# Gated recurrence in the scan stage: its input product and its output sum on GpSimd, the running sum left on VectorE

## What the reference computes

```
rg = sigmoid(block_diag_linear(xc, wa, ba))
ig = sigmoid(block_diag_linear(xc, wx, bx))
log_a = -8 * rg * softplus(-lam)
a  = exp(log_a)
bt = sqrt(-expm1(2 * log_a)) * (ig * xc)
h[t] = a[t] * h[t-1] + bt[t]          # in each direction; latents start from the context's last h
out  = (h_forward + h_backward) * gelu(gb) @ w_proj_lru
```

## Time and profile before

| what | value |
|---|---|
| median of 3 runs | 4300.68 us (4300.09 to 4311.89) |
| the profiled execution: time, span | 4309.31 us, 4307.5 us |
| granted TensorE clock, mean share of full speed | 0.93 |
| busy over the span: PE, DVE, ACT, POOL | 83%, 56%, 44%, 29% |
| scan stage | 1142 to 2402 us, a body every 66 to 73 us |

### The profile page before, as it was taken

One profiled execution on the slowest core, in us unless ns is written; L12 is line 12 of the kernel. 1 busy time (PEld: TensorE's weight loads), 2 busy tenths in 40 slices (PEclk: granted clock), 3 DMA queues, 4 the chain that ended last, 5 costly groups with the idle time before them and its releaser, 6 DMA issues. The chain is left out here.

```text
span 4307.5 us, 117683 instructions
## 1 busy us (share of the span) xinstructions
PE 3596.5 (83%) x50061; PEld 3199.9 (74%) x50061; DVE 2432.9 (56%) x4389; ACT 1889.2 (44%) x3285; POOL 1258.8 (29%) x1250
## 2 busy tenths in 40 slices
PE   5799999999677777877777588894599999999992
PEld 2678888888577676777667488672499999999992
DVE  3237676510156666677767654435666666666664
ACT  3246665521154555555555443331244444444444
POOL 2223333311254655555553254000001010101110
PEclk8899999999898999999999799996699999999996
DMA  5235555532433333332331574431367676767675
GB/s 173 69 127 180 170 185 168 171 111 71 117 72 83 93 82 83 83 92 79 87 96 35 175 229 142 147 127 40 115 196 221 195 219 198 214 203 209 208 207 196
DMA packets 566343, 610.18 MB, mean 142 GB/s; under 512 B 65938, under 2 KB 471252, under 8 KB 564820
## 3 DMA queue, kind: packets, MB, share of 16 engines
q1 hardware_dynamic: 515540, 487.01, 36.9%
q0 software_dynamic: 21536, 76.56, 6.2%
q10 hardware_dynamic: 28768, 39.16, 2.8%
HBM read 443.09 MB, written 159.40 MB: 140 GB/s over the span
## 5 line engine op out<-in xcount | busy, mean ns | idle before, releaser
L339 DVE TENSOR_TENSOR moe_w_lo<-moe_w_lo_whole,moe_w_hi 128x2048 fp32r<-128x2048 f32 (+1 forms) x258 | 453.6, 1758 | 263.5 <-ACT moe_w_hi L517 188.0
L460 PE MATMUL moe_h<-moe_xt_hi,moe_w_hi 128*128 128x256 f32 x2048 | 582.0, 284 | 15.9 <-DVE moe_xt_lo L339 14.8
L460 PE MATMUL moe_h<-moe_xt_lo,moe_w_hi 128*128 128x256 f32 x2048 | 580.1, 283 | 0.6 <-issue 0.6
L460 PE MATMUL moe_h<-moe_xt_hi,moe_w_lo 128*128 128x256 f32 x2048 | 580.1, 283 | 0.0
L1792 PE MATMUL inward_pp<-u_u_hi,inward_w_hi 128*128 128x512 f32 (+1 forms) x1360 | 527.4, 388 | 20.8 <-POOL inward_w_lo L1952 20.8
L1792 PE MATMUL inward_pp<-u_u_lo,inward_w_hi 128*128 128x512 f32 (+1 forms) x1360 | 515.7, 379 | 0.0
L1792 PE MATMUL inward_pp<-u_u_hi,inward_w_lo 128*128 128x512 f32 (+1 forms) x1360 | 515.5, 379 | 0.0
L460 PEld LDWEIGHTS moe_h<-moe_xt_hi,moe_w_hi 128*128 128x128 f32 x2048 | 393.2, 192 | 27.9 <-issue 23.7
L460 PEld LDWEIGHTS moe_h<-moe_xt_lo,moe_w_hi 128*128 128x128 f32 x2048 | 393.3, 192 | 3.7
L460 PEld LDWEIGHTS moe_h<-moe_xt_hi,moe_w_lo 128*128 128x128 f32 x2048 | 393.3, 192 | 1.1 <-issue 0.8
L412 POOL DMA_INDIRECT scratch_x<-moe_ys,moe_who x32 | 70.6, 2205 | 912.2 <-DVE moe_ys L568 907.4
(11 more groups left out here) (374 smaller groups left out, 9832.1 us busy)
## 6 DMA issues: line engine op xcount, KB each, us to landing
moe_w_lo_whole<-in_moe_w SPq DMA_DIRECT2D x387, 512.0 KB, 5.0
scratch_ops<-inward_ops SPq DMA_DIRECT2D x72, 514.0 KB, 3.8
scan_over<-scratch_ops SPq DMA_DIRECT2D x72, 512.0 KB, 9.9
inward_w_lo_whole<-in_w_in SPq DMA_DIRECT2D x38, 512.0 KB, 4.6
scan_aq<-scratch_ops SPq DMA_DIRECT2D x36, 516.0 KB, 5.0
scratch_gates<-inward_out SPq DMA_DIRECT2D x64, 256.0 KB, 2.2
all_late<-in_w_mod POOLq DMA_DIRECT2D x32, 512.0 KB, 4.5
rest_modsum<-scratch_gates SPq DMA_DIRECT2D x64, 256.0 KB, 4.4
```

What stands on the lines that cost most here:

```text
L339: return nc.vector.tensor_tensor(x_lo, x, x_hi.bitcast(F32), ALU.subtract)
L460: mm = nc.tensor.matmul(hb[ft % 2][m][:, 0:CAP], w_, x, start=(k == 0 and part == 0), stop=(k == KD - 1 and part == 2))
```

## The change

ScalarE's square root gets a scale of 0.25, so that the factor 0.5 of the "in" product is inside the root. The "in" product moves to GpSimd (`inputs`), as a plain product; the copy or addition into `z` moves to GpSimd (`summed`); VectorE's `recur` keeps the scan. New waits: the scan for the product, the output sum for the scan, ScalarE's `gates`, `squares` and `store_z` for the output sum. GpSimd's loop is written in another order. The diff, cut to its core:

```
-        DVs, POl = lru("scanned", ["in", "scan", "add"]), lru("pool", ["large", "one"])
+        DVs, POl, POi, POz = lru("scanned", ["scan"]), lru("pool", ["large", "one"]), lru("inputs", ["in"]), lru("summed", ["add"])
...  (gates, squares and store_z on ScalarE)
-                    DVs.wait(act, "scan", k - RING)
+                    POz.wait(act, "add", k - RING)
...
-                    act.activation(root[:, a:e, :], root[:, a:e, :], ACT.Sqrt).then_inc(s_root, 1)
+                    act.activation(root[:, a:e, :], root[:, a:e, :], ACT.Sqrt, scale=0.25).then_inc(s_root, 1)
...
             def store_z(j):
-                DVs.wait(act, "add", 2 * NG * (j + 1) - 1)
+                POz.wait(act, "add", 2 * NG * (j + 1) - 1)
...  (recur on VectorE)
-                dve.wait_ge(s_root, sum(1 + (4 * it % RING > 2) for it in range(k // 4 + 1)))
-                DVs.did("in", dve.scalar_tensor_tensor(out=x, in0=gated[:, k % RING, :], scalar=0.5, in1=x, op0=ALU.mult, op1=ALU.mult))
-                DVs.wait(dve, "in", k)
+                POi.wait(dve, "in", k)
+                if m:
+                    DVs.wait(dve, "scan", k - 1)
...
                 DVs.did("scan", dve.tensor_tensor_scan(x[:, way], decay[:, k % RING, way], x[:, way], start, ALU.mult, ALU.add))
...
-                    DVs.did("add", dve.tensor_copy(piece, h))
-                else:
-                    DVs.did("add", dve.tensor_tensor(piece, piece, h, ALU.add))
...  (new on GpSimd)
+            def inputs(k):
+                x = root[:, k % RING, :]
+                pool.wait_ge(s_root, sum(1 + (4 * it % RING > 2) for it in range(k // 4 + 1)))
+                POi.did("in", pool.tensor_tensor(x, x, gated[:, k % RING, :], ALU.mult))
+            def summed(k):
+                DVs.wait(pool, "scan", k)
+                if d == 0:
+                    POz.did("add", pool.tensor_copy(piece, h))
+                else:
+                    POz.did("add", pool.tensor_tensor(piece, piece, h, ALU.add))
...
+                more, first, past = it <= LAST, 4 * (it - 1), 4 * (it - 2)
+                squares(first)
+                inputs(past)
+                inputs(past + 1 if past >= 0 else -1)
                 if more:
                     start_solve(it)
-                squares(first)
+                    level(1, it)
+                summed(past)
+                summed(past + 1 if past >= 0 else -1)
                 if more:
                     level(2, it)
                 squares(first + 1 if it else -1)
+                inputs(past + 2 if past >= 0 else -1)
+                inputs(past + 3 if past >= 0 else -1)
                 if more:
                     level(3, it)
+                summed(past + 2 if past >= 0 else -1)
+                if more:
                     level(4, it)
                 squares(first + 2 if it else -1)
                 if more:
                     level(5, it)
+                summed(past + 3 if past >= 0 else -1)
                 squares(first + 3 if it else -1)
```

More of the change, by code:

```diff
@@ L2151, in scan @@
         none = n.sb("none", [P, 4])
+        spare = n.sb("spare", [P, 1])
         level_pe = [x for m in LEVELS for x in (f"F{m}", f"W{m}", f"T{m}")][:-1]
@@ L2784, in level @@
                     PO[u].did(f"H{m}", pool.tensor_tensor(four(H[u][(m - 1) % 3][:, :, :]), four(L[u][:, :, :]), masked(f"lev{m}t"), ALU.mult))
+            def inputs(k):
+                if k < 0:
+                    return
+                x = root[:, k % RING, :]
+                pool.wait_ge(s_root, sum(1 + (4 * it % RING > 2) for it in range(k // 4 + 1)))
+                POi.did("in", pool.tensor_tensor(x, x, gated[:, k % RING, :], ALU.mult))
+            def summed(k):
+                if k < 0:
+                    return
+                j, d, m, i = lru_of(k)
+                x = root[:, k % RING, :]
+                DVs.wait(pool, "scan", k)
+                if m == 0:
+                    POz.did("add", pool.memset(spare[:, :], 0.0))
+                    return
+                piece = z.rearrange("p (r w) -> p w r", w=GRID_W)[:, 8 * i:8 * i + 8, :]
+                h = x.rearrange("p (w r) -> p w r", r=GRID_H)
+                if d == 0:
+                    if m == 1 and j:
+                        pool.wait_ge(s_z, 16 * j)
+                    POz.did("add", pool.tensor_copy(piece, h))
+                else:
+                    POz.did("add", pool.tensor_tensor(piece, piece, h, ALU.add))
             def squares(k):
@@ L2796, in _ @@
                 PO[u].start(pool)
-            POl.start(pool)
+            for s in (POl, POi, POz):
+                s.start(pool)
             pool.wait_ge(s_masks, 16)
@@ L2801, in _ @@
             for it in range(LAST + 2):
-                more, first = it <= LAST, 4 * (it - 1)
+                more, first, past = it <= LAST, 4 * (it - 1), 4 * (it - 2)
+                squares(first)
+                inputs(past)
+                inputs(past + 1 if past >= 0 else -1)
                 if more:
                     start_solve(it)
-                squares(first)
+                    level(1, it)
+                summed(past)
+                summed(past + 1 if past >= 0 else -1)
                 if more:
-                    level(1, it)
                     level(2, it)
                 squares(first + 1 if it else -1)
+                inputs(past + 2 if past >= 0 else -1)
+                inputs(past + 3 if past >= 0 else -1)
                 if more:
                     level(3, it)
+                summed(past + 2 if past >= 0 else -1)
+                if more:
                     level(4, it)
@@ L2819, in _ @@
                         count = add(2 * it + half, count)
+            for k in range(4 * LAST, 4 * LAST + 4):
+                inputs(k)
+            for k in range(4 * LAST, 4 * LAST + 4):
+                summed(k)
 def backbone_layer(nc, t, out, scratch):
```

## The result

| | before | after |
|---|---|---|
| median (range), us | 4303.47 (4300.09 to 4311.89), 6 runs | 4332.69 (4321.43 to 4338.76), 6 runs |
| ratio with 95% interval | | 1.0057 [1.0043, 1.0071] |
| span and granted clock of the profiled execution | 4307.5 us, 0.932 | 4327.9 us, 0.923 |

The change costs 0.57%, 25 us of 4305. That is more than the 13 us that the prediction took as "no change". By the ratio it is inside the prediction's range of 4272 to 4330 (4300.7 x 1.0057 = 4325); the bare median, 4332.69, lies 2.7 us above it.

The account below looks back on a forecast made before the run. No engine is full in the scan stage; a body is a chain of waits through several queues. 15 bodies x (-1.0 - 0.2 + 1.2) = 0, and +3 once, on 4300.7: 4304 us, range 4272 to 4330.

Parts of the forecast that it names:

- rival C: GpSimd's queue becomes the bound: output sum takes 1.5 us or more, delaying q3 and T update by 2.0; 4328; chance 0.16.
- The stall absorbs part of the relief: First half of a body: of the 2.0 us wait for Z removed, -1.0 us a body survives TensorE's stall before chunk 2.
- H1 costs at most 0.3 us ... and the wait of unit 1 covers that: First half, GpSimd's H1 behind products and four additions: at most 0.3 us on unit 0, covered; uncovered, 0.5 us a body.
- The second half, +1.2 a body: After VectorE's S update, q3 waits for GpSimd's output sum, H4 and `squares`; W update late: +1.2 us a body, range +0.6 to +2.0.
- The output sum: GpSimd's copy or addition into z, price unknown: 0.9 us taken, 1.5 the upper bound for the addition.
- Taps, -0.2: VectorE's chunk 0 taps run with GpSimd idle, giving back the 3.3 us Lk wait: -0.2 us a body.
- `store_z`, +3 once: `store_z` of k = 35 holds ScalarE until the sum of a body's last piece, behind H5: once some 3 us.
- Its point of decision: The GpSimd-queue rival decides from the point at which q3 starts more than 1.2 us late.
- Rival D: Lock between engines: VectorE's two-input operations stretch while GpSimd works beside taps of chunks 1 and 3; +12 us, 4316; chance 0.10.

Follow-up runs that it names:

- sum_behind: The changed kernel with the third piece's output sum behind H4 and `squares` in GpSimd's queue instead of ahead of them: 4318.89 us, 1.0018 to the kernel before.
- relief_only: The kernel before with input product and output sum left out on every engine, z zeroed once: 4299.6 us, 0.9977 to the kernel before.
- small_load_relief: The kernel before with the operand reload cut to 16 columns per tile, and input product and output sum left out: 4183.5 us, 0.9701 to before.
- dummies: The kernel before, VectorE's work whole, plus GpSimd in the changed order doing products and plain copies on private tiles: 4324.39 us, 1.0025 to before.
- placed: The changed kernel with products 1, 2 back on VectorE, GpSimd's other new work behind H4 and H5, `store_z` two chunks later: 4312.37 us, 0.9997 to before.

## Why the prediction was right or wrong

It said 4304, no change by its bound. By the ratio the kernel came to 4325: inside the range, but 25 us slower than before, beside rival C's 4328. The range held by errors in both directions, and the number of C was met without its reason, so that is in part luck. The ledger in us, predicted and measured; sum_behind and relief_only share a chip:

| term | predicted | measured | from |
|---|---|---|---|
| relief, with the taps | -18 | -10 | relief_only |
| GpSimd's new work apart from q3: H1, contention | 0 | +18 | sum_behind over relief_only |
| q3 and the W update late | +18 | +17 | after over sum_behind |
| `store_z` | +3 | not seen apart | |
| sum | +3 | +25 | |

The measured terms are steps from one kernel to the next, so they add up by construction; each has an interval of 4 to 8 us to each side.

- **The stall absorbs part of the relief: right, undersized.** -1.0 a body was taken, the middle of 0 and -2.0; S2 came 0.7 sooner, and all of the relief is worth 10 / 15 = 0.67. That it absorbs is shown by small_load_relief. The Trainium skill ("Runtime: NRT & Kernel Launch", Instruction fetch mechanics) has block crossings mostly hidden, and by it the term would have been -2.0. The relief was worth 1.5 a body only where the reload was small.
- **"H1 costs at most 0.3 us ... and the wait of unit 1 covers that": this step failed.** The prices of the products were right (742 ns for 0.8), and the additions behind them begin 13.5 us into the body, as worked out. But the four additions were priced at 1.26 each, 5.0 together, and take 5.8 from the first to the last (means 1447 and 1491 ns, 1278 and 1277 before). H1 is done at 20.7 and 22.1 us of the body, not at 1706.0 - 1686.2 = 19.8 and 21.1. So F1 waits 11.8 us in all for H1, starts 0.5 a body later than before, and S1 is reached 1.0 later than in relief_only. That the relief took the cover away is not the reason: in dummies, without relief, F1 waits 12.6. The prediction named 0.5 a body for a missing cover and gave it no chance. Whether the delay costs time is another matter: in dummies the stall takes it back before S2.
- **The second half, +1.2 a body: the wait was foreseen, its size about right.** The order of GpSimd's queue, q3's start (5.91 us after the S update for 5.7 to 6.0) and F4's wait are as described. The W update is 9.71 - 8.07 = 1.64 later, where 8.9 - 7.5 = 1.4 was worked out for one body and 1.2 taken. Two errors in that partly cancel: the mark of before was one body with 7.5 (the mean is 8.07), and q3 was priced at 0.45 where it takes 1.43 beside an H product. S2 to S3 got 1.83 longer, 1.40 of it F4's wait. The low clock in 8 of 15 bodies, which the prediction never considered, is a small part of the rest. Over the whole kernel sum_behind shows 17 us for the term of 18: close, with part of what S2 to S3 lose not arriving at the end.
- **The output sum: sized right.** 0.9 was taken, 733 and 999 ns were measured.
- **Taps, -0.2:** the group fell from 135.9 to 131.2 us and TensorE's wait for Lk is not in the list, but the last part of the body (S3 to the end) got 0.25 longer, within its scatter, so no gain is seen to arrive.
- **`store_z`, +3 once:** ScalarE stands for it in three bodies, not one, 4.0 to 5.2 us each and 9.3 us more in all than before. What of that reaches the time, no run shows: placed issues it later and changes more besides.
- **Rival C** had the number and not its reason: the output sum is not 1.5 us or more. Its point of decision, q3 over 1.2 us late, was passed: 5.91 - 4.53 = 1.4.
- **Rival D** is in the result as a part. The Trainium skill ("SBUF — State Buffer", two separate sides) has an exclusive lock held for a whole instruction. The rows agree that operations stretch on both sides (q3 515 to 925 ns, T0 and W0 from 1278 to 1447 and 1491), and VectorE got back all the busy time that it gave. Its price on the path can't be told from H1's: placed, with H1 on time, is 9 us below sum_behind by the ratios, but on another chip and with less work on GpSimd, and the traces of both reach S2 at the same 42.85.

Open stays how the 18 us split between H1, contention and `store_z`, and what the clock costs by itself: no run holds the wait and not the clock. By the bodies it is 8 x 0.1 to 8 x 0.6, some 1 to 5 us.

## What to carry to other kernels

Where work is moved to an engine with an in-order queue, list what stands behind each new instruction and let it follow whatever another engine is waiting for: one output sum moved behind H4 and `squares` was worth 17 us. Before counting a wait that goes as a gain, look for the next stall and ask what it hangs on; a stall tied to a transfer takes the gain back until that is moved. And price an operation by rows taken beside the work that will run with it: the four additions priced at 5.0 us took 5.8, and the q3 priced at 0.45 took 1.43.

## What the hardware showed beyond that

Six transfers of SyncE in a block (2.62 MB in 13 us, DMA engines at 92.9%) go with a stall of TensorE of 4.6 us a body on the mean, at which no wait for an operand shows. Spreading the same transfers over the body gave 0.9%, cutting them to 16 columns 2.5%. Nothing in the list of waits names it: it stands there as "issue". In all 15 bodies of before it ends 2.5 to 3.0 us after the start of a 16 KB instruction packet, and in dummies, where TensorE came to it 1.0 us later, it was 1.0 us shorter.

Where F4 waited longest for the W update (2.14 us on the mean, 1.00 in the other bodies), in 8 of 15 bodies, the lower clock level followed; most of the 1.3 us by which these bodies are longer up to the next step S is the wait itself. An output sum moved on GpSimd, with nothing changed on TensorE, brings the clock in the window 8 to 12 us behind the S update back from 0.81 to 1.00.

Raster order on GpSimd: a copy of 128x256 took 554 ns between plain tiles (dummies) and 733 into `z`; a plain two-input operation took 742 ns and the addition in `z` 999.
